# Projections and expert queries of a two-block transformer kernel: fp32 products replaced by three fp32r products of split operands

## What is computed

```python
def first_block(x, c, ...):
    mod = c @ w_ada[l] + b_ada[l]                      # 1024 x 3072
    shift, scl, gate = jnp.split(mod, 3, axis=-1)
    h = rms_norm(x, g_norm[l]) * (1.0 + scl[:, None, :]) + shift[:, None, :]
    proj = h @ w_in[l]                                 # 1024 x 5120
    ...                                                # pooling, 8 heads of causal attention
    y_pool = y_pool @ w_pool_up[l]                     # 512 x 1024
    y_attn = y_attn @ w_attn_up[l]                     # 512 x 1024
    merged = jax.nn.sigmoid(m_pool) * y_pool + jax.nn.sigmoid(m_attn) * y_attn
    x = x + gate[:, None, :] * (merged @ w_out[l])
    return rms_norm(x, g_final)

def second_block(x, c, ...):
    mod = jax.nn.silu(c) @ w_ada[l] + b_ada[l]         # 1024 x 6144
    sh1, sc1, ga1, sh2, sc2, ga2 = jnp.split(mod, 6, axis=-1)
    h = _modulate(_rms_norm(x, g_norm_mix[l]), sh1, sc1)
    proj = h @ w_in[l]                                 # 1024 x 3352
    ...                                                # retention, compressed and windowed attention
    mix = jnp.concatenate([ret_out, nsa_out], axis=-1) @ w_out[l]
    x = x + ga1[:, None, :] * mix
    h = _modulate(_rms_norm(x, g_norm_ffn[l]), sh2, sc2)
    x = x + ga2[:, None, :] * _peer(h, w_peer_q[l], peer_subkeys[l], peer_down[l], peer_up[l])
    return _rms_norm(x, g_norm_final)

def _peer(...):                                        # per block of tokens
    q = (hblk @ w_q).reshape(B, TB, PEER_HEADS, 2, PEER_DHALF)   # 1024 x 2048
    ...                                                # top 16 of 16 x 16 pairs of keys
    a = jax.nn.gelu(jnp.einsum('btd,btpkd->btpk', hblk, w_down[eidx]))
    return jnp.einsum('btpk,btpkd->btd', w * a, w_up[eidx])
```

## Time and profile before

| | us |
|---|---|
| median of 3 runs | 1410.75 |
| lowest and highest | 1407.55, 1412.11 |
| the profiled execution | 1412.18 |
| its span, from the first to the last instruction | 1409.6 |
| mean granted TensorE clock, as a share of full speed | 0.96 |
| PE busy in the span | 1324.0 |
| DVE, ACT, POOL busy | 862.3, 466.2, 336.1 |

### The profile page before, as it was taken

How to read it: one execution, slowest core, us unless ns; L and a number is a source line. 1 busy time by engine, 2 the same in 40 slices (tenths; PEclk the granted TensorE clock), 3 DMA queues, 4 the chain that set the end, 5 groups by cost and what they waited for, 6 DMA issues and landing times.

```text
span 1409.6 us, 17917 instructions
## 1 busy us (share of the span) xinstructions
PE 1324.0 (94%) x7022; PEld 1040.5 (74%) x7022; DVE 862.3 (61%) x1594; ACT 466.2 (33%) x893; POOL 336.1 (24%) x150
## 2 busy tenths in 40 slices
PE   5899999969989797999898999999999999999997
PEld 1444555437745556899898999999998888888885
DVE  3545542244363622079998399999986666666666
ACT  1012110001112311054443544443345555555553
POOL 0000000000000000058989766666640000000000
PEclk9999999978688989999999999999999999999999
DMA  9876662226253112235565544444446666666664
GB/s 378 339 284 275 264 265 87 93 91 237 111 222 135 62 60 81 98 112 178 161 180 154 175 137 148 136 139 147 135 150 194 194 194 194 194 195 194 192 193 152
DMA packets 54514, 244.19 MB, mean 173 GB/s; under 512 B 6944, under 2 KB 7328, under 8 KB 42016
## 3 DMA queue, kind: packets, MB, share of 16 engines
q1 hardware_dynamic: 54000, 242.34, 49.8%
q10 hardware_dynamic: 432, 0.72, 0.2%
HBM read 240.94 MB, written 2.10 MB: 172 GB/s over the span
## 4 chain that ended last, share of the span: by engine, by line
PE 87%; DVE 6%; POOL 3%; issue 1%; ACT 1%; DMA 1%; SPq 0%; POOLq 0%; DVEq 0%
PE bank L779 21%; PE bank L1112 8%; PE bank L1079 8%; PE bank L1115 8%; PE bank L1118 8%; PE bank L1076 8%; PE bank L1075 8%; PE bank L1088 4%; PE bank L1046 4%; POOL split_r L554 3%; PE bank L968 2%; PE bank L788 1%; DVE tab L1192 1%; PE bank L771 1%; PE bank L889 1%
## 5 line engine op out<-in xcount | busy, mean ns | idle before, releaser
L554 POOL TENSOR_TENSOR split_r<-ring,split_r 128x1024 fp32r<-128x1024 f32 x128 | 326.3, 2553 | 182.8 <-ACT split_r L711 182.2
L711 ACT ACTIVATE split_r<-ring 128x1024 fp32r<-128x1024 f32 x256 | 269.2, 1052 | 245.8 <-PE bank L1079 245.8
L779 PE MATMUL bank<-G 128*128 128x512 f32 (+1 forms) x608 | 270.2, 604 | 6.5 <-DVE G L1300 4.1
L1075 PE MATMUL bank<-h_high_r,split_r 128*128 128x256 f32 x1024 | 256.2, 288 | 1.7 <-ACT split_r L711 1.7
L1076 PE MATMUL bank<-h_low_r,split_r 128*128 128x256 f32 x1024 | 250.8, 283 | 0.0
L779 PEld LDWEIGHTS bank<-G 128*128 128x128 f32 x608 | 118.1, 197 | 149.2 <-issue 147.7
L1568 DVE TENSOR_TENSOR split_r<-ring,split_r 128x1024 fp32r<-128x1024 f32 x128 | 156.9, 1225 | 66.6 <-ACT split_r L711 66.6
L1075 PEld LDWEIGHTS bank<-h_high_r,split_r 128*128 128x128 f32 x1024 | 195.9, 191 | 1.9 <-issue 1.9
L1076 PEld LDWEIGHTS bank<-h_low_r,split_r 128*128 128x128 f32 x1024 | 196.4, 192 | 0.0
L1079 PE MATMUL bank<-h_high_r,split_r 128*128 128x256 f32 x1024 | 144.9, 284 | 9.3 <-POOL split_r L554 9.3
L1079 PEld LDWEIGHTS bank<-h_high_r,split_r 128*128 128x128 f32 x1024 | 131.9, 192 | 11.5 <-POOL split_r L554 11.5
(11 more groups left out here) (231 smaller groups left out, 1365.4 us busy)
## 6 DMA issues: line engine op xcount, KB each, us to landing
ring<-in_down SPq DMA_DIRECT2D x128, 512.0 KB, 3.5
ring<-in_up SPq DMA_DIRECT2D x128, 512.0 KB, 3.5
G<-in_ada SPq DMA_DIRECT2D x36, 1024.0 KB, 11.1
G<-in_in SPq DMA_DIRECT2D x32, 1024.0 KB, 7.1
G<-in_out SPq DMA_DIRECT2D x8, 1024.0 KB, 8.3
G<-in_wq SPq DMA_DIRECT2D x8, 1024.0 KB, 7.1
G<-in_poolup SPq DMA_DIRECT2D x2, 1024.0 KB, 6.1
G<-in_attnup SPq DMA_DIRECT2D x2, 1024.0 KB, 10.1
```

Of the source, the lines that this page charges most:

```text
L554: pool.tensor_tensor(wsplit[:, j % SPLIT, 1, :], raw[:, j % RAW, :], wsplit[:, j % SPLIT, 0, :].bitcast(F32), ALU.subtract).then_inc(low_r ...
L711: nc.scalar.activation(wsplit[:, n % SPLIT, 0, :], raw[:, n % RAW, :], ACT.Copy).then_inc(high_ready, 1)
L779: ins = mm(bank[:, 0:cols], lhs[c], rhs[c], start=(c == 0), stop=(c == n - 1))
L1075: mm(o, w[0][:, c, :], h_high[:, c, :], start=(c == 0), stop=False)
```

## The change

Every product of `project` and `peerq` is made from split operands, as the experts' are. The panels are halved: `STREAM` holds halves of 1 MB (four chunks of 512 columns), and there are eight slots of 1 MB. A half of weights takes a pair of slots: it is loaded into the first, ACT writes its high half (fp32r) into the second (`panel_split`), and then POOL, or DVE for five of the 54 halves, writes raw minus high over the raw weights (`low`, 512 columns at a time; `panel_rest`, 2048 at once). There are three such pairs; modulation halves use the two slots that are left. The modulated activations are split likewise (`x_split` on ACT, `x_rest` on DVE), and so are the transposed inputs of the up and output projections (`y_split`, `y_rest`). PE multiplies a half for both token tiles in three rounds of 8 products (`products`).

`proj`, `up` and `wout` always use banks 0 and 1, `peerq` too, everything else banks 2 and 3, and a panel of projections fills both banks before either is emptied. The modulation sums are cut in halves as well, partial sums stand in PSUM banks 4 and 5, and the table `SUM_AT` says behind which half of weights (counted from 0) each of the 28 sums stands that are not part of the start: 12 behind the first ten panels, 4 in the first block's up and output projections, 6 behind the second block's first three panels, 2 behind `hid`, 4 in the expert queries. The start now sums `ada1` 1 on DVE, a row no longer. `HIGH_AT` sets where in `STEPS` ACT rounds each half. For keys and values of the second block's attention the copies by POOL are gone (PE writes two of the four transposes twice itself), and one half silu, pooling and the last transposes have moved a few places.

```diff
+FIRST = 3
+SUM_AT = [0, 1, 3, 5, 6, 8, 10, 11, 13, 15, 16, 18, 21, 22, 24, 25, 28, 29, 30, 31, 32, 33, 33.5, 33.5, 46, 47, 49, 51]
...
+    at, w = [], -1
+    for n, s in enumerate(weights):
+        w += s[3] == "pe"
+        out.append(s)
+        while len(at) < len(sums) and w >= (0 if len(at) < 2 else SUM_AT[len(at) - 2] + 2) and s[3] == "pe":
+            out.append(sums[len(at)])
+            at.append(n)
...
+        elif user == "dve":
+            at[n] = 6 + turn % 2
+            turn += 1
+        else:
+            at[n] = 2 * pairs.pop(0)
+            pairs.append(at[n] // 2)
+        used = [at[n]] if user == "dve" or n < SLOTS else [at[n], at[n] + 1]
+        before[n] = [last[k] for k in used if k in last]
...
+LOW_BY_VECTOR = [AT["in1", IN1[0], 0], AT["in2", 5, 0], AT["in2", 5, 1], AT["wq", 0, 0], AT["wq", 0, 1]]
+PIECE = 512
+LOW_BY_POOL = [n for n in SPLITS if n not in LOW_BY_VECTOR]
...
+    for w, n in enumerate(SPLITS):
+        users = [step_of[m] for m in BEFORE[n] if m in step_of] + ([step_of[SPLITS[w - 2]]] if w >= 2 else [])
+        latest = max([latest] + users)
+        at.setdefault(latest, []).append(n)
+    return at
+
+
+HIGH_AT = high_steps()
...
+            for n, (name, i, h, user) in enumerate(STREAM):
+                for b in BEFORE[n]:
+                    half_used(sp, b)
+                src, words = d[name] if i is None else d[name][i], WORDS.get(name, HALF)
...
+            def low(names):
+
+                for n in LOW_BY_POOL:
+                    if STREAM[n][:3] in names:
+                        lo, raw_, hi = low_half(pool, n)
+                        words = WORDS.get(STREAM[n][0], HALF)
+                        for c in range(0, words, PIECE):
+                            part = slice(c, min(c + PIECE, words))
+                            ins = pool.tensor_tensor(lo[:, part], raw_[:, part], hi[:, part], ALU.subtract)
+                        ins.then_inc(panel_low, 1)
+
...
+            def panel_split(n):
+
+                words = WORDS.get(STREAM[n][0], HALF)
+                src = wait_half(act, n)[:, 0:words]
+                nc.scalar.activation(slot_r[SLOT_OF[n] + 1][:, 0:words], src, ACT.Copy).then_inc(panel_high, 1)
...
+                for n in HIGH_AT.get(k, ()):
+                    if n != SPLITS[0]:
+                        panel_split(n)
+                if kind == "xT" and s[2:] == (0, 0):
+                    b = s[1]
+                    act.wait_ge(mod_ready, b + 1)
+                    modulate(b, 0)
+                    x_split(b, 0, 0)
+                    x_split(b, 1, 0)
+                    modulate(b, 1)
+                    x_split(b, 0, 1)
+                    x_split(b, 1, 1)
...
+            def products(n, outs, x_high_, x_low_, chunks, first, last):
+
+                k = SLOT_OF[n]
+                words = WORDS.get(STREAM[n][0], HALF)
+                hi, lo = (slot_r[m][:, 0:words].rearrange("p (c n) -> p c n", c=4) for m in (k + 1, k))
+                if first:
+                    for s, _, _ in outs:
+                        bank_to_fill(pe_, s)
+                pe_.wait_ge(panel_high, SPLITS.index(n) + 1)
+                for part in (x_high_, x_low_):
+                    for s, o, tok in outs:
+                        for c in range(4):
+                            mm(o, part[:, chunks + c, tok], hi[:, c, :], start=(first and part is x_high_ and c == 0), stop=False)
+                wait_low(pe_, n)
+                for s, o, tok in outs:
+                    for c in range(4):
+                        ins = mm(o, x_high_[:, chunks + c, tok], lo[:, c, :], start=False, stop=(last and c == 3))
+                    if last:
+                        bank_full(ins, s)
+                if not last:
+                    ins.then_inc(part_used, 1)
+
             pe_.wait_ge(first_in, 16)
...
+            def column_sum(k, half):
...
+                a = total if k < FIRST else ps[4 + k % 2][:, :]
...
+                    if half == 0 and c == 0:
+                        ins = ts(a, w[:, 0, :], col_, None, ALU.mult)
+                    else:
+                        ins = stt(out=total if half == 1 and c == 3 else a, in0=w[:, c, :], scalar=col_, in1=a,
+                                  op0=ALU.mult, op1=ALU.add)
+                    if c < 3:
...
+            def x_rest(b, k):
+
+                half, t = divmod(k, 2)
+                dve.wait_ge(x_high, 4 * b + k + 1)
+                evacuated(dve, ("xT", b, t, half))
+                part = (slice(None), slice(4 * half, 4 * half + 4), slice(t * P, (t + 1) * P))
...
+            def panel_rest(n):
+
+                lo, raw_, hi = low_half(dve, n)
+                tt(lo, raw_, hi, ALU.subtract).then_inc(panel_low_dve, 1)
...
+                elif kind == "half" and s[1:] == ("out1", 1, 1):
+                    panel_rest(AT["in2", 5, 0])
+                elif kind == "half" and s[1:] == ("out2", 1, 1):
+                    panel_rest(AT["wq", 0, 0])
+                elif kind == "xT" and s[2:] == (0, 0):
+                    b = s[1]
+                    modulate(b, 0)
+                    modulate(b, 1)
+                    for k in range(4):
+                        x_rest(b, k)
+                        if k == 1 and b == 0:
+                            panel_rest(AT["in1", IN1[0], 0])
+                    if b:
+                        panel_rest(AT["in2", 5, 1] if b == 1 else AT["wq", 0, 1])
```

699 lines of the change are left out of this document (390 added, 309 removed).

## The result

The changed kernel takes 1451.1 us (median of 4 runs, 1449.07 to 1452.75), the kernel before 1409.15 (4 runs, 1406.96 to 1412.11): a ratio of 1.0296, 95% interval 1.0268 to 1.0323. Forecast were 1375 us, and slower by over 0.3% had a chance of 0.12. The profiled execution spans 1447.3 us where before it spanned 1409.6; the experts take the same 800 us, so all 37.7 us of the difference lie ahead of them.

What follows compares the result with a forecast made beforehand. Before the experts, PE's work mostly bounds, DMA at the start, with PE waiting for softmax and DVE sums among the heads. Stage terms −1 + 20 + 10 − 8 − 0.5 + 22 − 1 give 41.5 us gained, less 5: 1375 us, range 1340 to 1408.

Steps and rivals of the forecast that it cites:

- the 5 us set aside for clock and contention: Set against the 41.5 us gained, for PE's new gaps at 299 to 338 and 570 and its lower granted clock.
- Prices: Costs per instruction: fp32r product 0.227 us against 0.87 float32, POOL piece 1.22, ACT rounding 1.91, half sum 3.1.
- POOL's rival: POOL is the bound: pieces of 1.75 to 2.2 us, deciding from 1.65 at 75 to 202; 1425 us, chance 0.11.
- 0.8 us for seven panels: 75 to 202 us: PE waits 0.8 us per panel for ACT to empty banks after load and rounding; stage 107 us.
- The start: 0 to 75 us: PE starts at 46 instead of 41, the stretch ends at 76; 1 us lost.
- 281 to 338 us: After the second block's norm DVE is the limit with 42 us of work; 65 us in place of 57, 8 lost.
- "20 gained" from the panels: 370 to 533 us: eight halves of `in2` 0 to 3 take 43.6 us where token tiles took 7.13 to 9.86 each.
- 12 from modulation products: 370 to 533 us: four modulation panels leave the heads' stretch, two of them stood in the chain; 12 us gained.
- 202 to 281 us: Eight halves at 43.6 us, with transpositions rounded and subtracted between and the softmax's end; 69 us, 10 gained.
- The wait in the queries: 533 to 609 us: PE waits 7 us because the fourth half of `wq` loads behind a modulation half; stage 77 for 76.
- The rival "lower clock stays": At 299 to 338 and between light heads products run at half speed, costing 25 to 30 us; 1400 us, chance 0.09.
- The port: DVE instructions with two SBUF inputs and POOL's block each other for whole instructions; estimated 9 us, giving 1384, left out of 1375.

Runs made afterwards that it cites:

- run 3: Changed kernel with modulation loads issued by ACT instead of SP, and ACT emptying a panel's banks before rounding a half: 1414.1 us, ratio 1.0029.
- Run 10: run 3 plus two pairs of banks used in turn, sums kept in SBUF, and the three gate loads one panel sooner: 1389.6 us, ratio 0.9859.
- run 5: run 3 with DVE's modulation sums placed behind its work on a panel's two banks: 1418.1 us, ratio 1.0076.
- run 13: Run 10 with eight half sums moved from the stretch ahead of the compressed keys to between the heads: 1382.6 us, ratio 0.9820.
- Run 9: run 3 with panels taking two pairs of banks in turn and the modulation sums kept in SBUF: 1395.9 us, ratio 0.9901.
- Run 12: Run 10 with 14 of 24 products in each half of `in2` 0 to 3 left out: 1382.7 us, ratio 0.9806.
- run 11: Run 10 with float32 products of projections and queries, small activation parts left out, weights neither rounded nor subtracted: 1419.3 us, ratio 1.0065.
- Run 8: run 3 with POOL subtracting a half in one instruction of 2048 columns instead of four of 512: 1430.1 us, ratio 1.0150.
- run 1: Changed kernel with modulation loads issued by ACT, so that SP issues weight halves alone: 1427.3 us, ratio 1.0113.
- run 2: Changed kernel with ACT rounding a half only behind the two copies that empty the banks: 1422.2 us, ratio 1.0092.
- run 4: Changed kernel with float32 products of loaded halves by rounded activations, weights neither rounded nor subtracted, order of loads and sums kept: 1444.8 us, ratio 1.0241.

## Why the prediction was wrong, step by step

The forecast was 36.5 us under the profiled execution before; it came out 37.7 over: 74 us. By stage, misses against the sum: start 10, `in1` 4 to 9 32, out1 2, `in2` 5 to 4 8, hid 3, sixteen heads and out2 23, queries 1.6; that is 79, of which the 5 us set aside for clock and contention were to cover a part. (Worked out exactly, the sum gives 1375.7 against the profiled execution and 1374.3 against the median, not 1375.5 and 1375; nothing hangs on it.)

- **Prices held.** POOL's piece was taken at 1.22 us; it took 1.29 in the median, 1.32 in the mean. Rounding took 1.91 us as in the earlier trace rows, half sums 3.0 for 3.1, 16 fp32r products 3.63 at full clock. PE started at 46.3, as forecast (46). POOL's rival (1425, from 1.65 us a piece) did not decide: the pieces stayed under its 1.65.
- **75 to 202 us: the step "0.8 us for seven panels".** It let a half be late only by its own load (4.9 us) and rounding, taking DVE's sums as done in time. That overlap failed: four loads, each directly behind a modulation half's, were issued 2.8 to 7.9 us late, since DVE reached the sum only behind an output that waits for PE. The load itself was mis-sized where another went directly ahead: 4.9 had been worked out, 4.8 us stands in the chain for one with no other directly ahead of it (at 92.23), but 6.9 for one behind a modulation load (at 112.43), and 6.2 in the median; the page of the kernel before, not used for this, has 7.1 for `in_in`, two at a time. PE stood for 24 us in this stage where 5.6 had been allowed, and its work took 114 us, not 101, at a clock of 0.88. With the coupling cut and the banks first, the stage took 104 us (run 3) where 107 had been forecast.
- **The start.** ACT rounded the second half at 41.3, as forecast, but the wait of DVE for the gate loads (15.8 us, once, from 62.0 to 77.8), ahead of its next half sum and of the rotation, was not in the forecast at all. Run 10 gives this back: 73.5 us, under the 76 forecast.
- **281 to 338 us.** "DVE is the limit" was right (runs 5 and 13), 8 us lost came out as 17. The forecast had 42 us of DVE's work, but not the place of the six half sums in the order: PE stood for 5.4 and 7.8 us (327.7 and 342.1) while DVE summed and rotated, since a single pair of banks left nothing to fill. The prediction wrote down both facts and priced only their total. Run 9 gives 9 us back.
- **370 to 533 us: "20 gained" from the panels and 12 from modulation products.** This is where the method failed. The prediction says itself that PE waits there for the softmax and for sums on DVE, yet I subtracted the saved work from the length as if PE, busy 115 of 129 us in the earlier trace rows, were the limit. Run 12 shows that 25 us less of products are worth 4.9 there, and runs 10 and 11 that float32 products cost it only 4.5 (169.7 against 165.1), though PE is busy 14.5 us more. PE's busy time had products at the lower clock in it, and when work is taken away the clock falls further (0.83 to 0.73 in run 12). The stretch took 165 to 180 us in all variants that make all products, 169.9 before.
- **202 to 281 us, the queries**: 72.1 for 70, 77.6 for 76. The wait in the queries was there, as forecast: the chain has 7.28 us of load and 1.91 of rounding, and again 5.13 and 1.91, and PE stood for 5.0 and 1.6 us where 7 had been said.
- **The clock.** It was lower where PE waited (0.88 for 1.00 in `in1` 4 to 9) and came back in run 3. The rival "lower clock stays" (1400) had the kind right, lower clock behind PE's waits, and named 299 to 338 and the light heads, where it was 0.79. It did not have the waits of `in1` 4 to 9, where the clock cost 13 us of PE's work.
- **The port.** The Trainium skill's rule (SBUF — State Buffer, Who interferes with whom) was priced at 9 us and left out. Run 8 bears it out. At the start of the changed kernel two subtractions of DVE (L1445, from 49.41 us) took 3.46 us together beside POOL's pieces, where the same two in run 3, with POOL idle, took 1.28. Its whole share in the 74 us was not measured.

What is shown: the loads' queue and ACT's order (runs 1 to 3, 37 us together), the single pair of banks (18 us behind them, 32 alone), the gate loads (6), DVE's sums ahead of the compressed keys (7), the worth of the products with their splitting (30). These overlap and don't add. What stays open: what sets the sixteen heads (steps of the softmax, DVE's sums or light products at the lower clock), why they take 8 us more in run 3 than in the changed kernel, and how much of the 74 us is the port's.

## What to carry to other kernels

Where PE was busy for all of a stretch (127 of 127), saved work became saved time once loads and banks kept up (104 in run 3); where it was busy for 90%, it did not, and there a run that leaves products out tells more than any sum. When work is cut in halves to make it cheaper, list for each new load what stands ahead of it in its queue and who frees that slot, and for each pair of banks who empties it and what that engine does first; a wait of 0.8 us on paper became 6.4 to 8.8 at three panels, where the queues of SP, ACT and DVE, each worked off in order, closed a ring with PE. An arrangement that only serves a cheaper instruction should be timed with the old instruction in it (runs 4 and 11): the 35 us of cost were there before the products entered.
